# Where the sample's units stand among the prompt's in the stick-breaking phase

## The reference, cut to what matters

```
z = q @ k.T * d ** -0.5
log_beta = log_sigmoid(z)
log_rest = where(causal, log_sigmoid(-z), 0)
suffix = reverse_cumsum(log_rest) - log_rest
A = where(causal, exp(log_beta + suffix), 0)
o = A @ v
```

## Time and profile before

| what | value |
| --- | --- |
| median of the three runs | 3358.83 us (3356.28 to 3361.95) |
| the profiled execution, its own time | 3362.2 us |
| its span, first to last instruction | 3360.5 us |
| mean granted TensorE clock | 0.950 of full speed |
| PE / PEld / DVE / ACT / POOL busy | 90% / 74% / 42% / 29% / 26% of the span |
| stick phase, first scan to last | 1540.4 to 2462.9 us |

### The profile page before, as it was taken

The page is one execution under the profiler, slowest core; times in us unless marked ns, Lnnn a source line. Parts: engine busy times, 40 slices in busy tenths (PEclk is TensorE's granted clock), DMA queues, the critical chain, the costliest instruction groups (busy, mean ns, idle before and its releaser), DMA issues. The chain is left out here.

```text
span 3360.5 us, 50789 instructions
## 1 busy us (share of the span) xinstructions
PE 3019.1 (90%) x19627; PEld 2499.5 (74%) x19627; DVE 1417.4 (42%) x2011; ACT 989.5 (29%) x1827; POOL 872.7 (26%) x846
## 2 busy tenths in 40 slices
PE   5799999999999999986988988989968956999798
PEld 5688888888888888874766766766747734977687
DVE  4431111000000000007997997988956612533333
ACT  3551111111111111104454444444537823200121
POOL 4241121111111111102433433434425510433100
PEclk8899999999999999997998999999979966999899
DMA  4322222221222212218457456544546523744443
GB/s 170 110 74 73 94 87 72 70 76 65 73 70 71 73 68 73 69 47 226 159 161 208 155 166 206 164 148 158 165 128 185 169 67 91 222 159 155 168 136 113
DMA packets 308291, 415.55 MB, mean 124 GB/s; under 512 B 26577, under 2 KB 186961, under 8 KB 307697
## 3 DMA queue, kind: packets, MB, share of 16 engines
q1 hardware_dynamic: 276320, 310.76, 30.1%
q0 software_dynamic: 31760, 101.87, 8.3%
HBM read 309.93 MB, written 102.63 MB: 123 GB/s over the span
## 5 line engine op out<-in xcount | busy, mean ns | idle before, releaser
L385 PE MATMUL prj_bank<-hidden_hi,prj_w_hi 128*128 128x512 f32 (+2 forms) x2320 | 833.5, 359 | 9.9 <-DVE prj_w_lo L439 9.9
L387 PE MATMUL prj_bank<-hidden_hi,prj_w_lo 128*128 128x512 f32 (+2 forms) x2320 | 829.4, 357 | 0.0
L386 PE MATMUL prj_bank<-hidden_lo,prj_w_hi 128*128 128x512 f32 (+2 forms) x2320 | 829.1, 357 | 0.0
L385 PEld LDWEIGHTS prj_bank<-hidden_hi,prj_w_hi 128*128 128x128 f32 x2320 | 437.5, 189 | 64.5 <-DVE prj_w_lo L439 10.3
L429 ACT ACTIVATE prj_z<-prj_bank 128x512 f32<-128x512 f32 x290 | 155.0, 534 | 1112.5 <-PE prj_bank L387 1112.2
L387 PEld LDWEIGHTS prj_bank<-hidden_hi,prj_w_lo 128*128 128x128 f32 x2320 | 437.3, 188 | 55.1
L386 PEld LDWEIGHTS prj_bank<-hidden_lo,prj_w_hi 128*128 128x128 f32 x2320 | 437.6, 189 | 53.6
L437 DVE CAST prj_w_hi<-prj_w 128x1024 fp32r<-128x1024 f32 x58 | 40.2, 693 | 893.1 <-PE prj_bank L387 882.1
L901 POOL TENSOR_TENSOR stk_beta<-stk_beta,stk_left 128x1024 f32<-128x1024 f32 (+4 forms) x160 | 282.4, 1765 | 478.1 <-DVE stk_left L816 478.1
L486 POOL DMA_DIRECT2D scratch_zT<-prj_z x240 | 130.8, 545 | 981.7 <-ACT prj_z L429 964.9
L765 ACT ACTIVATE stk_beta<-stk_z 128x1024 f32<-128x1024 f32 (+2 forms) x224 | 181.8, 812 | 350.8 <-PE stk_z L952 272.6
(11 more groups left out here) (226 smaller groups left out, 4425.1 us busy)
## 6 DMA issues: line engine op xcount, KB each, us to landing
stk_kd<-in_cache_sb_k SPq DMA_DIRECT2D x64, 1024.0 KB, 7.1
stk_vd<-in_cache_sb_v SPq DMA_DIRECT2D x64, 1024.0 KB, 5.3
scratch_zT<-prj_z POOLq DMA_DIRECT2D x144, 256.0 KB, 2.3
prj_w<-in_w_in SPq DMA_DIRECT2D x58, 512.0 KB, 3.8
mrg_gate<-scratch_zT SPq DMA_DIRECT2D x24, 768.0 KB, 4.4
scratch_zT<-prj_z POOLq DMA_DIRECT2D x48, 192.0 KB, 2.1
mrg_u_raw<-scratch_uT SPq DMA_DIRECT2D x9, 1024.0 KB, 9.1
fin_a_raw<-scratch_mgT SPq DMA_DIRECT2D x17, 512.0 KB, 4.7
```

The lines of the kernel that those rows point to most:

```text
L385: pe.matmul(out, w_hi[u][:, k, :], hi[:, k, first:first + width], start=k == 0, stop=False)
L386: pe.matmul(out, w_hi[u][:, k, :], lo[:, k, first:first + width], start=False, stop=False)
L387: last = pe.matmul(out, w_lo[u][:, k, :], hi[:, k, first:first + width], start=False, stop=k == KC - 1)
```

## The change

```diff
     prompt = [("p", t, b) for t in range(NT) for b in range(t // 4, -1, -1)]
     decode = [("d", b, k) for b in (0, 1) for k in range(PAST // 512, -1, -1)]
-    cost = [min(4, t + 1 - 4 * b) for _, t, b in prompt]
+    cost = [1 for _ in prompt]
     trailing = 2
```

## The result

| | before | changed |
| --- | --- | --- |
| median of four runs each, us | 3359.35 (3356.28 to 3361.95) | 3404.76 (3402.07 to 3406.06) |
| the profiled execution, its own time | 3362.2 | 3405.23 |
| its span | 3360.5 | 3403.6 |
| mean granted TensorE clock | 0.950 | 0.946 |

The changed kernel takes 1.0137 times as long, interval 1.0124 to 1.015: 45.4 us slower. The prediction said slower by 18, and its range ended at 3391. So the sign was right and the size was not, by 27 us.

A forecast was written before the change was run, and what follows sets the result against it. PE and VectorE, both near full, wait for each other by turns. Joints +9, round 0's start -1 and terms 3 to 5 +10 sum to +18 us: 3380, or 3377 against the median; range 3361 to 3391.

The forecast's parts named there:

- Joints: Three places where rounds meet: PE stops for the new keys with less work done beforehand; +9 us, from 5 to 13.
- The +2.5 up to the gate: At each joint, work PE did before its wait for new keys now follows it, ending 2.5 us later.
- The +0.5 for what comes behind the jump: Behind the loop's jump, d0.7 at step 6 makes PE need VectorE just as it returns; 0.5 us a joint.
- Start of round 0: Up to p5.1 and d0.7, most of VectorE's 1.62 us wait for an output goes; -1 us, from -2 to 0.
- A scan behind a full unit: Scans of p10.0, p11.0, p12.0, p14.1 wait for GpSimd: 3.7 us a round against 2.3 before, so +1.4 a round.
- The credit for the narrow units of before: In the old order, scans of p8.2, p9.2 and p12.3 wait for GpSimd; 2.3 us a round saved.
- half speed for both: Alternative for VectorE and GpSimd sharing bandwidth: four full units lose 0.4 us each, the sum about 8 us lower.
- Behind d1.7: p12.1's scans wait 2.4 us for GpSimd where p13.3's lost 1.37; +1.0 us a round.
- PE behind: PE late behind cache blocks: d1.6's step some 1.0 us longer, 0.9 credited elsewhere; +0.1 together, from -1.5 to +1.5.
- The credit of 0.9 for other places: Waits at d0.6 and beside it, where PE came late behind narrow units, were to go; 0.9 us.
- Loads carry no term: Cache blocks are asked for two blocks ahead, some 24 us, the same within a step or two; no cost.
- PE gets the bound: Rival: a round's first half runs at PE's pace, the second has VectorE alone; about +35 us, 3394; chance 0.10.

The follow-up runs named there:

- the short products: Changed order, with GpSimd multiplying only the first 128 keys of the units ahead of p10.0, p11.0, p12.0 and p14.1: 3386.42 us, ratio 1.0078.
- the two kernels that keep TensorE busy: Changed order, with second weight transpositions repeated: d1.7's 6 or 12 times more, d0.1's and d1.4's 3 times more: 3396.53 us (6) and 3396.27 us (12).

## Why the prediction was wrong in size

By its own terms, against the 47.4 us that the stick phase grew in the trace:

1. **Joints, +9 forecast: about 12 measured** (six traces of each order; 13.6 in the pair of traces above). The bounds of 5 to 13 held it. The +2.5 up to the gate was right, to the tenth by luck: PE's wait grew to 6.2, not 7.5, and the work behind it took longer instead. The +0.5 for what comes behind the jump was too small: it is 1.5 at the first joint, where PE makes d0.7's keys at the lower clock. The cause, the new keys behind a waiting load, was right: with the keys first 0.9 us of the term are left.
2. **Start of round 0, -1: -0.6, and -1.2 by the six traces of each order.** Right.
3. **A scan behind a full unit, +1.4 a round: each scan right, the sum not.** 3.7 a round was forecast for the four full units and 3.66 measured by the short products. The credit for the narrow units of before was of the right size too: p8.2's and p9.2's steps were 2.67 and 3.21 and are 2.03 and 2.36 now, 1.5 for two of the three, where 2.3 was forecast for all three. By the Trainium skill ("SBUF — State Buffer", section "Who interferes with whom") the engine that issues second fully blocks; the runs agree, with 3.50 for 2.45 here and 2.45 again once GpSimd's work was short. GpSimd's instruction, which came first, keeps its 2.00 beside the 3.50. That tells the lock from half speed for both, not the length of the scan: at half speed GpSimd would have taken longer and the scan would have lost as much, so the prediction's 0.4 for that case was worked out wrongly. What the term missed is that other scans get free in the new order, those of cache blocks and first blocks: over steps 9 to 57 all scans together take 1.4 us less in four rounds than before, where terms 3 and 4 had +2.4 a round.
4. **Behind d1.7, +1.0: not to be told apart.** p12.1's scan is blocked for 1.0 (3.47) where 2.4 were forecast, and p13.3's is free now (1.27 for 2.62) as forecast, but p13.3's step isn't shorter (4.32 for 3.79 in three rounds).
5. **PE behind, +0.1 a round: this is the step that failed.** Outside the first nine steps VectorE's idle time grew from 62.4 to 93.8 us, 7.8 a round, and the rounds there by 8.6 each where terms 3 to 5 had 2.5. Steps 33 to 38 alone grew by 4.05 a round, 16 us, and 3.7 of that appear when these six steps alone are put into the old order (+15.5 us). The prediction noted that d1.8 moves, counted copies and scans around it, and never asked what PE has to do while VectorE has two light units in a row. Half of that growth is VectorE waiting for PE. At d1.6 the size of +1.0 was right (4.35 against 3.16 as a usual step), but not by the narrow unit ahead of it: with d1.6 behind p13.3 in the old order its step is 2.65. The credit of 0.9 for other places didn't come. Why TensorE is as late as it is from step 39 on, where VectorE's idle time grows from 9.0 to 30.6 us, no run isolates.

**"Loads carry no term" was wrong too**, by up to 3 us: p6.0's step is 5.79, 7.45, 7.22 and 6.57. In rounds 1 and 2, 3.1 us above the first, PE waits there for cache keys (0.94 and 0.77, the 1.7 in the list above); in round 3 it doesn't. The blocks' distance was counted in mean steps over a round, and the early steps are not mean ones. This I read from the trace; no run was made with these loads earlier.

**Left out altogether: the clock**, some 8 us by the two kernels that keep TensorE busy, with the wide interval given there. Since PE was near full in the kernel before and its clock at 1.00 inside the rounds, the prediction took all durations at the upper level for granted.

Taken one at a time, the experiments give 12.3 us for the joints, 15.5 for steps 33 to 38, 18.6 for the four blocked scans and some 8 for the clock. These overlap (p12.0's scan is one of the four and lies in steps 33 to 38, and a wait brings the lower clock with it), so they don't add up to a ledger of the 47.4; by kind it is VectorE's idle time, 42.1, nearly whole. The rival "PE gets the bound" had the mechanism, and at 3394 the nearest figure of all; it looked for it in the first half of a round, where it is small, and got 0.10. The 4.3 us less in the rest of the program are scatter: outside the stick phase the fourteen traces take 2429 to 2438 us, and that of before is at the upper end.

## What to carry to other kernels

When an order of units is changed, walk through it with both engines' lists side by side: at each step, what the other engine owes from several steps back, against what this one has to do in that time. Two light units in a row are light for one engine only. And when a blocked instruction is priced, look for the one that gets free in its place, and for the wait that was hidden under it: here the scans took 1.7 us more in all and the idle time 42.1. Before pricing a wait at a joint, see what issues the load that it waits for; here two lines in the load queue were worth more (-11.6 us) than any order tried. And a range made of the terms' own bounds leaves out the term that nobody wrote: short waits have a second price, the clock behind them.

## What the hardware showed unexpectedly

- The granted TensorE clock falls in the middle of a dense phase beside short waits. By an idle time of 3.30 us that ends at 1930.56 it reads 0.51 from 1930 on and is back at 1.00 by 1934; eight transpositions take 1.97 us in it, 1.09 outside. With repeated transpositions in that wait it reads 1.00 throughout. The shortest wait beside which it fell was 1.58 us; eleven others of 1.3 us or more between the joints left it at 1.00.
- A unit's step reproduces from round to round and from kernel to kernel to some 0.02 us as long as its neighbours are the same: 93.0 and 54.3 us in each of four rounds of the kernel before, p12.2's 6.96 in each of the changed kernel. So a loss of a few us can be placed in a trace long before a median tells it. The joints are the exception: steps 0 to 8 of the old order sum to 142.4 to 146.2 in six traces.
- TENSOR_TENSOR_SCAN on VectorE and TENSOR_TENSOR on GpSimd block each other in whichever order they come: 3.50 or 3.31 for 2.45 when the scan is second, and in the kernel before 3.14 for 2.00 when GpSimd is the earlier trace rows. Which scans are blocked depends on the order of units: the sum of all of them hardly moved.
